# One streamed conditioning product in eight units with a ring of eight loads, its gate product moved into the next stream

## The chip, the cores and the metric

The kernel runs on one core of one Trainium2 chip. The metric is the device time of one execution in microseconds, as the median of several executions. For the kernel before it is 2430.32 us (three runs, 2429.95 to 2431.19).

## The reference, cut to what matters

One layer of a mixed recurrent network is computed for 288 tokens: a prompt of 256 tokens and 8 sequences of 4 sample tokens. All of it is float32, the model width D is 2048.

```python
mod = silu(c) @ ada_w + ada_b                # c: 1 + 8 rows of 2048, ada_w: 2048 x 12288
sh1, sc1, g1, sh2, sc2, g2 = split(mod, 6)
h = rms_norm(x) * (1 + sc1) + sh1
proj = h @ w_in                              # 2048 x 18448: heads q, f, i, g, ..., and 8 + 8 gate columns
...                                          # HGRN2 and mLSTM heads, w_out, residual
h = rms_norm(x) * (1 + sc2) + sh2
...                                          # ConvFFN with w_up and w_down, residual, final norm
```

The change is about the first line for sh1 and sc1 (columns 0 to 4095 of ada_w, 33.6 MB), the first rms_norm, and the product of h with the 16 gate columns of w_in (input and forget gates of the mLSTM heads, C_MI and C_MF).

## The kernel before, in words

**Weights in chunks.** Every weight matrix is streamed once from HBM. A chunk is four contraction tiles of 128 rows by 256 columns (KC = 4, CN = 256): one DMA of 512 KB on SP's queue, in rows of 1 KB, into one of four slots of `raw` (RING = 4). For a chunk of w_in, ACT rounds it to float32r (`hi`, L878, tile `whi`), DVE takes the rest (`lo`, L1239, tile `wlo`), and PE multiplies (`chunk`, L523 to L525): per contraction tile and half of 128 columns three matmuls over 288 tokens, whi with xh, whi with xl, wlo with xh, 24 in all. xh and xl are the two parts of the normalised, modulated input. A `stage` on SP, and a `stream` on PE, ACT and DVE, walk through the same list of kinds: "s" is such a chunk, "a" is a chunk of ada_w for the later conditioning vectors, which goes into `araw` and takes four matmuls (`ada_chunk`, L534: 32 columns of `cs` against 256 columns, one contraction tile in each quarter of the output's partitions). The program's float32 matmuls show as two rows each in the trace.

**The first conditioning product.** Before the first stream, `ada1_stream` takes the 64 chunks for sh1 and sc1 through `raw`: per turn i of 8 eight chunks, four for each of two banks. After four chunks ACT copies the 128 x 256 partial sums out (`ada_rows_of`, L881), PE adds the four quarters with `sel` and transposes (`ada_turn`, L541, two matmuls of 128 columns), and DVE adds the bias (L1254). SP loads chunk k when the chunk four places earlier has been used (`ada1_stage`). In the first four turns PE also transposes the inputs (`xtm`, L502, three per contraction tile, 16 tiles), ACT copies them to `xT` (L949) and squares them (L952), and POOL adds the squares up (L1653). Then one matmul with ones (L629) makes the mean squares, and ACT makes rstd. ACT's queue loads c, x, the parameter rows (`partm`), the gate columns (`gw`), three gate constants and `cvr`, in this order, before its first computation.

**Between this product and the first stream.** When all of mod is there, DVE adds 1 to the scales (L1302) and for each of four groups of contraction tiles multiplies by rstd (L1311) and modulates the samples (L1314, L1316), ACT modulates the prompt (L932) and rounds to xh (L938), and DVE takes xl (L1306). PE then multiplies the 16 gate columns, 8 at a time (L640 to L642, 96 matmuls), and starts the first stream, `stream(hg_base(0), HG_KINDS, A_HG)`, of 40 "s" and 12 "a" chunks. While PE works on its first three chunks, ACT and DVE compute the rows of the gates, which need the gate product (ACT L976 to L986, DVE L1333 to L1356); their loops over the fourth and later chunks come behind these in program order. After the first stream PE transposes the gate rows (L502 on `merged`).

The lines that set the order before the first stream are these:

```python
pe.wait_ge(landed[k % RING], 4 * ada1_base(i)[0] + 16 * (k // RING + 1))
ada_chunk(raw[:, k % RING], s == 0, s == 3, ps[:, b, 0, :], KC * s).then_inc(used, 1)
...
for k in range(8):
    if not first or k >= RING:
        sp.wait_ge(used, ada1_base(i)[0] + k - RING + 1 + FREE)
    load(k, ada_v, KC * (k % 4), 512 * i + CN * (k // 4))
```

Of the kernel before, what the change touches and what calls it, by code (L numbers as in the profile page):

```python
# [21 lines left out]
P = 128  # L22
# [23 lines left out]
CONST_ALL = 37  # L46
SEL_DONE = 11
# [5 lines left out]
CN = 256  # L53

# [15 lines left out]
N_ADA1 = (0, 0)  # L70


# [5 lines left out]
def ada1_base(i):  # L78
    return ahead(N_ADA1, i, 8, 1)


N_HG = (64, 8)
# [36 lines left out]

A_HG = 16  # L120
# [22 lines left out]
HG_TURNS = (2, 11, 20, 29)  # L143
HG_TURNS_ML = (1, 8, 16, 23)
# [14 lines left out]
def build(nc, x_prompt, x_sample, c_prompt, c_sample, state_hgrn, state_mlstm_C, state_mlstm_n, state_mlstm_m,  # L159
# [5 lines left out]
    with ExitStack() as ctx:  # L165
# [8 lines left out]
        whi = sb("whi", [P, RING, KC, CN], F32R)  # L174
        wlo = sb("wlo", [P, RING, KC, CN], F32R)
# [47 lines left out]
        arows1 = sb("arows1", [P, CN], stack=setup)  # L223
        arows = (arows0, arows1)
# [3 lines left out]
        ctm = sb("ctm", [NB, D], stack=setup)  # L228
        cvr = sb("cvr", [2 * FT, NS, P], stack=setup)
        partm = sb("partm", [P, 4, P], stack=setup)  # L230
        gw = sb("gw", [P, KT, 2 * MH], stack=setup)
        gwh = sb("gwh", [P, KT, 2 * MH], F32R, stack=setup)
        gwl = sb("gwl", [P, KT, 2 * MH], F32R, stack=setup)
# [91 lines left out]
        a_used = sem("a_used")  # L325
        ada_rows = sem("ada_rows")
# [5 lines left out]
        par_t, par_c = sem("par_t"), sem("par_c")  # L332
        c_zero, c_silu, c_t, c_c = (sem(n) for n in ("c_zero", "c_silu", "c_t", "c_c"))
        cv_t, cv_c = sem("cv_t"), sem("cv_c")
        x_t, x_c, x_sum = sem("x_t"), sem("x_c"), sem("x_sum")
# [92 lines left out]
        def _(sp):  # L428
# [20 lines left out]
            def ada1_stage(i, first=False):  # L449
                for k in range(8):  # L450
                    if not first or k >= RING:
                        sp.wait_ge(used, ada1_base(i)[0] + k - RING + 1 + FREE)
                    load(k, ada_v, KC * (k % 4), 512 * i + CN * (k // 4))
# [10 lines left out]
            ada1_stage(0, first=True)  # L464
            with sp.Fori(1, 8) as i:
                ada1_stage(i)
# [31 lines left out]
        def _(pe):  # L498
# [38 lines left out]
            def ada_turn(n, half, acc):  # L537

                pe.wait_ge(ada_rows, n + 1)
                for m in range(2):  # L540
                    x = mm(acc[:, CN + NB * m:CN + NB * (m + 1)], arows[half][:, P * m:P * (m + 1)], sel[:, :], start=True, stop=True)  # L541
                x.then_inc(ada_cols, 1)
# [12 lines left out]
            def stream(N, kinds, a0=None, steps=None, length=4, kt0=0, xparts=None, halves=None, a_ring=araw):  # L555

                steps = nothing() if steps is None else steps
                for k, kind in enumerate(kinds):
                    if kind == "s":
# [7 lines left out]
                        chunk(N[0] - N_HG[0] + q + 1, q, s == 0, s == length - 1, b % 2, xh, xl, kt0 + KC * s, steps, halves if q == 0 else None)  # L567
                    else:
                        e = before(kinds, k, "a")
                        if e % 4 == 0:  # L570
                            pe.wait_ge(ada_free, a0 - A_HG + e // 4 + FREE)
                        pe.wait_ge(a_landed[e % ARING], 16 // ARING * before_a(a0) + 16 * (e // ARING + 1))
                        ada_chunk(a_ring[:, e % ARING], e % 4 == 0, e % 4 == 3, ab, KC * (e % 4)).then_inc(a_used, 1)
                    if k >= 2 and kinds[k - 2] == "a" and before(kinds, k - 1, "a") % 4 == 0:
                        ada_turn(a0 + before(kinds, k - 1, "a") // 4 - 1, 0, ab)
                drain(steps)

            def ada1_stream(i, hook=None):

                for k in range(8):  # L580
                    b, s = k // 4, k % 4
                    if s == 0:
                        pe.wait_ge(bank_free[b], ada1_base(i)[1] + FREE)
                    pe.wait_ge(landed[k % RING], 4 * ada1_base(i)[0] + 16 * (k // RING + 1))
                    ada_chunk(raw[:, k % RING], s == 0, s == 3, ps[:, b, 0, :], KC * s).then_inc(used, 1)
                    if s == 1 and b:
                        ada_turn(2 * i, 0, ps[:, 0, 0, :])
                    if hook is not None:
                        hook(k)
                ada_turn(2 * i + 1, 1, ps[:, 1, 0, :])  # L590

# [3 lines left out]
            pe.wait_ge(const, 4)  # L595
            pe.wait_ge(ld_c, 32)
            pe.wait_ge(c_silu, 1)
            for kt in range(KT):
                x = tr(ab[:, NB * kt:NB * (kt + 1)], ctm[0:NB, P * kt:P * (kt + 1)])
            x.then_inc(c_t, 1)  # L600
            pe.wait_ge(ld_par, 16 * 9)
            for t, r in enumerate((128, 92, 88, 108)):
                x = tr(R[:, 2, P * t:P * t + r], partm[0:r, t, :])
            x.then_inc(par_t, 1)

            pe.wait_ge(const, SEL_DONE)
            pe.wait_ge(c_c, 1)
            pe.wait_ge(ld_x, 48)
            for i in range(4):
                def hook(k, i=i):  # L610
                    if k % 2:
                        kt = 4 * i + k // 2
                        pe.wait_ge(x_c, kt + X_FREE - 1)
                        for tt in range(3):
                            w = P if tt < 2 else TS
                            x = tr(R[:, k // 2 % 2, P * tt:P * tt + w], xtm[0:w, tt, P * kt:P * (kt + 1)])
                        x.then_inc(x_t, 1)
                ada1_stream(i, hook)
            pe.wait_ge(ld_conv, 16)
            for g in range(2):  # L620
                if g == 0:
# [1247 lines left out]
```

## Time and profile before

| | us |
|---|---|
| median of three runs | 2430.32 |
| the profiled execution, its own time | 2427.25 |
| its span | 2425.7 |
| granted TensorE clock, mean over the span | 0.966 of full speed |
| PE busy | 2298.0 |

The span is what the instruction records cover; the execution's own time is 1.55 us longer. Times within the profile count from the start of the span. L12 is line 12 of the kernel. "PEld" are weight loads of TensorE. The granted clock has two levels, 0.5 (1.2 GHz) and 1.0 (2.4 GHz); other values are means over a stretch. The share of the DMA engines is the mean over 16 of them of the time that their packets took; packets overlap, so it can be above 1.

### The profile page before, as it was taken

To read this page: it belongs to the slowest core of one execution; us is meant where nothing else is said; L and a number is where in the kernel's file an instruction comes from. 1 tells how busy PE (TensorE), PEld (TensorE's weight loads), DVE (VectorE), ACT (ScalarE), POOL (GpSimd) and SP (SyncE) were. 2 spreads that over 40 slices of the span, in tenths; PEclk is the share of its full clock that TensorE was granted. 3 is DMA by queue.
4 is the path that set the end of the run, shared out by engine and by line. 5 is a ranking of instruction groups with operands and counts; after the bars stand their busy time and mean duration, and the time that the engine had idled before them with its cause. 6 is when DMAs were issued, how large, how long until landed. Compare 5 with 4: busy or idle time off the path is not lost. (4 is left out here: it accounts for less than half of the span.)

```text
span 2425.7 us, 45810 instructions
## 1 busy us (share of the span) xinstructions
PE 2298.0 (95%) x17728; PEld 2101.1 (87%) x17728; DVE 1096.9 (45%) x1443; ACT 1016.2 (42%) x1377; POOL 331.2 (14%) x461
## 2 busy tenths in 40 slices
PE   5769999899899999999999997899999999999997
PEld 2249999899889888888888896899999999999997
DVE  0043446446346444443443555655454545544443
ACT  2244455345435433444343443544444434433332
POOL 2100022112122221112111214000000000010000
PEclk8579999999999999999999999999999999999998
DMA  8947665656566565665765656465666555555552
GB/s 265 303 156 217 198 190 188 194 175 196 174 188 202 173 213 172 199 228 179 236 211 185 193 167 211 149 200 183 197 191 199 186 163 165 184 181 165 163 168 83
DMA packets 425403, 460.15 MB, mean 190 GB/s; under 512 B 16671, under 2 KB 415111, under 8 KB 424029
## 3 DMA queue, kind: packets, MB, share of 16 engines
q1 hardware_dynamic: 410064, 409.26, 53.8%
q0 software_dynamic: 11408, 45.54, 5.7%
q10 hardware_dynamic: 3782, 3.14, 0.4%
q8 instruction: 122, 2.00, 0.3%
q14 instruction: 27, 0.22, 0.0%
HBM read 431.48 MB, written 26.39 MB: 189 GB/s over the span
## 5 line engine op out<-in xcount | busy, mean ns | idle before, releaser
L523 PE MATMUL ps<-xh,whi 128*128 128x288 f32 x3968 | 1203.1, 303 | 39.2 <-issue 28.4
L1239 DVE TENSOR_TENSOR wlo<-raw,whi 128x1024 fp32r<-128x1024 f32 x584 | 734.8, 1261 | 1033.8 <-ACT whi L878 1032.6
L524 PE MATMUL ps<-xl,whi 128*128 128x288 f32 x3968 | 1175.2, 296 | 0.0
L525 PE MATMUL ps<-xh,wlo 128*128 128x288 f32 x3968 | 1174.9, 296 | 0.0
L878 ACT ACTIVATE whi<-raw 128x1024 fp32r<-128x1024 f32 x584 | 615.8, 1057 | 885.3 <-PE ps L525 789.6
L523 PEld LDWEIGHTS ps<-xh,whi 128*128 128x128 f32 x3968 | 749.8, 189 | 110.9 <-issue 94.1
L524 PEld LDWEIGHTS ps<-xl,whi 128*128 128x128 f32 x3968 | 750.1, 189 | 5.9 <-issue 5.9
L525 PEld LDWEIGHTS ps<-xh,wlo 128*128 128x128 f32 x3968 | 749.6, 189 | 0.0
L523 PE MATMUL ps<-ffh,whi 128*128 128x288 f32 x704 | 209.5, 298 | 0.0
L525 PE MATMUL ps<-ffh,wlo 128*128 128x288 f32 x704 | 207.5, 295 | 0.0
L524 PE MATMUL ps<-ffl,whi 128*128 128x288 f32 x704 | 207.2, 294 | 0.0
L523 PEld LDWEIGHTS ps<-ffh,whi 128*128 128x128 f32 x704 | 132.2, 188 | 0.2
L525 PEld LDWEIGHTS ps<-ffh,wlo 128*128 128x128 f32 x704 | 132.1, 188 | 0.0
L524 PEld LDWEIGHTS ps<-ffl,whi 128*128 128x128 f32 x704 | 132.0, 188 | 0.0
L534 PE MATMUL ps<-raw,cs 128*32 128x256 f32 x512 | 61.6, 602 | 21.1 <-DMA raw<-in_ada_w 21.1
L1827 POOL COPY tails<-abuf 128x4 f32 x22 | 4.2, 189 | 446.4 <-ACT abuf L1190 446.4
L534 PE MATMUL ab<-araw,cs 128*32 128x256 f32 x768 | 61.3, 391 | 0.0
L534 PEld LDWEIGHTS ps<-raw,cs 128*32 128x32 f32 x512 | 14.5, 141 | 51.0 <-DMA raw<-in_ada_w 44.1
L1727 POOL TENSOR_TENSOR S<-S,AC 128x1024 f32<-128x1024 f32 x16 | 31.6, 1972 | 164.8 <-PE R L696 164.8
L1254 DVE TENSOR_TENSOR mod<-ps,par 128x18 f32 x16 | 2.8, 176 | 107.3 <-PE ps L541 107.3
L1196 ACT ACTIVATE ffh<-yb 128x576 f32 x22 | 15.1, 686 | 69.0 <-DVE yb L1556 69.0
L1549 DVE SCALAR_TENSOR_TENSOR acv<-abuf,par,acv 128x304 f32<-128x304 f32 x88 | 41.0, 527 | 0.0
(352 smaller groups left out, 1654.6 us busy)
## 6 DMA issues: line engine op xcount, KB each, us to landing
raw<-in_w_in SPq DMA_DIRECT2D x288, 512.0 KB, 4.9
raw<-in_w_up SPq DMA_DIRECT2D x176, 512.0 KB, 3.6
araw<-in_ada_w SPq DMA_DIRECT2D x96, 512.0 KB, 3.9
raw<-in_w_down SPq DMA_DIRECT2D x88, 512.0 KB, 3.6
raw<-in_ada_w SPq DMA_DIRECT2D x64, 512.0 KB, 5.1
raw<-in_w_out SPq DMA_DIRECT2D x32, 512.0 KB, 3.6
araw_up<-in_ada_w SPq DMA_DIRECT2D x32, 512.0 KB, 4.3
S<-in_state_hgrn POOLq DMA_DIRECT2D x16, 512.0 KB, 4.8
```

Of the source, the lines that this page charges most:

```text
L523: mm(o, whi[:, s, kk, cols], hi[:, kt0 + kk, :], start=first and kk == 0, stop=False)
L524: mm(o, whi[:, s, kk, cols], lo[:, kt0 + kk, :], start=False, stop=False)
L525: x = mm(o, wlo[:, s, kk, cols], hi[:, kt0 + kk, :], start=False, stop=last and kk == KC - 1)
L534: x = mm(acc[32 * kk:32 * kk + 32, 0:CN], cs[:, kt0 + kk, :], weights[:, kk, :], start=first, stop=last)
L878: A(whi[:, s], raw[:, s], ACT.Copy).then_inc(hi_done, 1)
L1196: A(ffh[:, bass.ds(2 * i, 2), :], yb[:, :, :], ACT.Copy).then_inc(ff_hi, 1)
L1239: TT(wlo[:, s], raw[:, s], whi[:, s].bitcast(F32), ALU.subtract).then_inc(lo_done, 1)
L1254: TT(mod[:, bass.ds(2 * n, 2), :], acc[:, CN:CN + 2 * NB].rearrange("p (m b) -> p m b", b=NB), rep_last(bias_row[:, bass.ds(2 * n, 2)], NB ...
L1549: STT(acv[:, m, 0:AB - 2], abuf[:, m, w:w + AB - 2], cw[w][:, c1], acv[:, m, 0:AB - 2], ALU.mult, ALU.add).then_inc(ff_conv, 1)
L1727: G(S0[:, :, :], S0[:, :, :], rep_last(AC[:, 3, j, :], P), ALU.mult).then_inc(hg["scaled"], 1)
L1827: nc.gpsimd.tensor_copy(tails[:, bass.ds(2 * i, 2), 0:2], abuf[:, :, TP:TP + 2]).then_inc(ab_tail, 1)
```

## The change

- The product for sh1 and sc1 is taken in 8 units of 512 columns, shift and scale in turn (`unit_tiles`): unit 0 is shift tiles 0 to 3, unit 1 scale tiles 0 to 3, and so on. A unit is eight chunks of the old shape (four contraction tiles by 256 columns, 512 KB, rows of 1 KB), loaded into a new ring of eight, `uraw`, which lies over `whi` and `wlo`; a semaphore counts each pair of chunks. SP loads a pair again when the same pair of the unit before has been used.
- A unit has one copy by ACT of 128 x 512, one turn of four matmuls by PE, and one addition of bias by DVE, with the 1 of the scales in it.
- `raw` is free in this stage. SP issues the first four chunks of the first stream, and the first two "a" chunks, without a wait, behind the last unit.
- PE sums the squares itself: 16 matmuls with ones over 288 tokens, four in each of units 1 to 4, in place of POOL's 16 additions and one matmul.
- The first rms_norm follows the units: DVE multiplies by rstd after unit 3, groups 0 and 1 are modulated after it, group 2 after unit 5, group 3 after unit 7.
- c goes in as rows of 128 values, on SP's queue ahead of the first unit (2 transposes in place of 16); the parameter rows go on SP's queue behind unit 0; the gate columns (now two loads of 8 columns, into columns 0 and 32 of a tile 40 wide), the gate constants and `cvr` go on POOL's queue behind its constants. ACT's queue has only x. `cs` is zeroed by POOL.
- The gate product is 48 matmuls with 40 columns, taken as steps inside the first stream from its chunk 5 on (GATES = 5); ACT and DVE compute the gate rows inside their loops at chunks 9 to 11, 14 and 15.

The diff, cut to its core:

```diff
@@ sync
+            def unit_load(u, c):
+                s = (UC * u + c) % URING
+                if u:
+                    sp.wait_ge(u_used, 4 * (u - 1) + c // 2 + 1)
+                sp.dma_start(uraw[:, s], ada_v[:, KC * (c % 4):KC * (c % 4 + 1), bass.ds(P * unit_tiles(u) + CN * (c // 4), CN)]).then_inc(u_landed[s // 2], 16)
-            ada1_stage(0, first=True)
-            with sp.Fori(1, 8) as i:
-                ada1_stage(i)
+            sp.dma_start(ctm[:, 0, :], c_sample.rearrange("b (k p) -> (b k) p", p=P)).then_inc(ld_c, 16)
+            sp.dma_start(ctm[0:KT, 1, :], c_prompt.rearrange("b (k p) -> (b k) p", p=P)).then_inc(ld_c, 16)
+            for c in range(UC):
+                unit_load(0, c)
...
+            for u in range(1, UNITS):
+                for c in range(UC):
+                    unit_load(u, c)
@@ stage
-                        if first and n < RING:
-                            sp.wait_ge(used, N[0] + n - RING + 1 + FREE)
-                        else:
-                            sp.wait_ge(lo_done, N[0] - N_HG[0] + n - RING + 1)
+                        if not first or n >= RING:
+                            sp.wait_ge(lo_done, N[0] + n - RING + 1)
@@ tensor
+            def unit(u, tiles):
+                acc = ps[:, u % 2, 0, :]
+                if u >= 2:
+                    pe.wait_ge(ada_rows, u - 1)
+                for h in range(UC // 2):
+                    pe.wait_ge(u_landed[h], 32 * (u + 1))
+                    for c in (2 * h, 2 * h + 1):
+                        for kk in range(KC):
+                            x = mm(acc[32 * kk:32 * kk + 32, CN * (c // 4):CN * (c // 4 + 1)], cs[:, KC * (c % 4) + kk, :], uraw[:, c, kk, :], start=c % 4 == 0, stop=c % 4 == 3)
+                    x.then_inc(u_used, 1)
+                    if h == 0 and u:
+                        unit_turn(u - 1)
+                    tiles(h)
+            def squares_sum(g):
+                pe.wait_ge(sq_done, g + 1)
+                for kt in range(4 * g, 4 * g + 4):
+                    x = mm(ab[:, 0:T], ones[:, :], merged[:, kt, :], start=kt == 0, stop=kt == KT - 1)
...
+                    if u == 0 and h == 0:
+                        pe.wait_ge(ld_x, 48)
...
+            def gates(j, o, n, i):
+                pe.wait_ge(gw_lo, 1)
+                pe.wait_ge(small_c, 5)
+                pe.wait_ge(xlo, 4)
                 for kt in range(KT):
...
+                    if kt % 2:
+                        yield
-            pe.wait_ge(cv_c, 2)
-            stream(hg_base(0), HG_KINDS, A_HG)
+            pe.wait_ge(ada_free, UNITS + FREE)
+            stream(hg_base(0), HG_KINDS, A_HG, late(GATES, gates(0, "", 0, 0)), xparts=0)
@@ scalar
+            for u in range(4):
+                unit(u)
+            act.wait_ge(const, 7)
+            root(1, ab[:, 0:T], 1.0 / D)
...
+            unit(4)
...
+            act.wait_ge(ld_gw, 32)
...
+            modulate(1, merged, 0, KT, (0, 1))
+            unit(5)
+            modulate(1, merged, 0, KT, (2,))
+            unit(6)
+            unit(7)
+            hi(N_HG, 0, True)
+            hi(N_HG, 1, True)
+            modulate(1, merged, 0, KT, (3,))
+            hi(N_HG, 2, True)
@@ vector
+            unit(6)
+            unit(7)
+            dve.wait_ge(ada_free, UNITS + FREE)
+            samples(1, merged, 3, 0, KT)
+            lo(N_HG, 0, True)
+            lo(N_HG, 1, True)
+            low_parts(1, merged, 3)
+            lo(N_HG, 2, True)
```

## Rows read from the trace of the kernel before

**Rows 1.** The page's busy times of PE, and its slices of the span.

```profile
PE 2298.0 (95%) x17728; PEld 2101.1 (87%) x17728; DVE 1096.9 (45%) x1443; ACT 1016.2 (42%) x1377; POOL 331.2 (14%) x461
...
PEclk8579999999999999999999999999999999999998
```

**Rows 2.** Busy time, granted clock, DMA share and GB/s in stretches before 200 us.

```profile
core 0: us, PE busy (x) PEld busy (x) DVE busy (x) ACT busy (x) POOL busy (x), PEclk, DMA share, GB/s
0.00:137.00 137.00, 89.24 (x642) 37.56 (x642) 5.75 (x25) 27.66 (x51) 23.04 (x60) 0.67 0.90 288
95.00:135.00 40.00, 30.87 (x220) 10.88 (x224) 1.06 (x6) 2.31 (x6) 0.00 (x0) 0.50 1.00 324
10.00:15.00 5.00, 0.00 (x0) 0.00 (x0) 0.00 (x0) 0.00 (x0) 2.33 (x10) 1.00 1.04 286
...
80.00:85.00 5.00, 2.29 (x14) 1.10 (x18) 2.18 (x6) 3.05 (x6) 3.66 (x5) 0.50 0.46 176
...
190.00:200.00 10.00, 10.00 (x80) 9.42 (x79) 4.90 (x4) 4.24 (x4) 0.00 (x0) 1.00 1.09 355
```

**Rows 3.** The timeline at the end of the conditioning product, up to the first stream.

```profile
137.34 0.25 PEld L534 LDWEIGHTS ps<-raw,cs 128*32 128x32 f32 x8 [0.60 <-DMA raw<-in_ada_w]
138.54 0.39 ACT L881 ACTIVATE arows<-ps 128x256 f32<-128x256 f32 x1 [6.54 <-PE ps L534]
138.98 1.02 PE L541 MATMUL ps<-sel,arows 128*128 128x9 f32 x4 [0.51 <-ACT arows L881]
...
152.60 0.40 PE L640 MATMUL R<-xh,gwh 128*8 128x288 f32 x1 [12.60 <-DVE xl L1306]
...
155.20 0.33 PE L642 MATMUL R<-xh,gwl 128*8 128x288 f32 x1
...
168.91 0.29 PE L523 MATMUL ps<-xh,whi 128*128 128x288 f32 x1
```

**Rows 4.** Groups of one engine's instructions by line: PE from 150 us, ACT and DVE before 180 us.

```profile
L641 PE MATMUL R<-xl,gwh 128*8 128x288 f32 x32 | 10.0, 313 | 0.0
L932 ACT ACTIVATE merged<-merged,mod 128x256 f32<-128x256 f32 x16 | 8.3, 587 | 2.9 <-DVE merged L1311 2.9
L878 ACT ACTIVATE whi<-raw 128x1024 fp32r<-128x1024 f32 x4 | 4.2, 1052 | 1.8 <-DMA raw<-in_w_in 1.8
L1239 DVE TENSOR_TENSOR wlo<-raw,whi 128x1024 fp32r<-128x1024 f32 x3 | 3.7, 1226 | 1.1 <-ACT whi L878 1.1
L1314 DVE TENSOR_TENSOR merged<-merged,mod 128x128 f32<-128x128 f32 x4 | 1.2, 292 | 0.1
```

**Rows 5.** The timeline around PE's stall in the first stream, and at its end.

```profile
178.56 0.64 PE L534 MATMUL ab<-araw,cs 128*32 128x256 f32 x8
181.59 0.40 PE L523 MATMUL ps<-xh,whi 128*128 128x288 f32 x1 [2.39 <-DVE wlo L1239]
...
310.97 0.72 PE L502 MATMUL R<-ident,merged 8*128 8x8 f32 x9
```

**Rows 6.** The chain that ended last, later in the kernel: one period of three chunks.

```profile
1535.38 0.57 PE ab L534 x8
...
1545.71 0.57 PE ab L534 x8
```

**Rows 7.** The timeline of PE's pieces of work during the conditioning product.

```profile
26.39 0.93 PE L502 MATMUL R<-ident,xtm 128*128 128x128 f32 x3
...
82.72 1.30 PE L629 MATMUL R<-lnms,ones 128*128 128x288 f32 x2 [3.24 <-POOL lnms L1653]
83.94 3.42 PE L534 MATMUL ps<-raw,cs 128*32 128x256 f32 x32
```

**Rows 8.** DMA issues by line: KB each, and us from issue to landing.

```profile
raw<-in_ada_w SPq DMA_DIRECT2D x64, 512.0 KB, 5.1
...
xT_spill<-xT POOLq DMA_DIRECT2D x2, 1152.0 KB, 6.5
gw<-in_w_in ACTq DMA_DIRECT2D x1, 128.0 KB, 10.9
```

More of the change, by code:

```diff
@@ L45 @@
 ROW_T = ROW_WK
-CONST_ALL = 37
-SEL_DONE = 11
+CONST_ALL = 39
+CONST_CS = 1
+SEL_DONE = 12
 X_FREE = 2
@@ L325, in build @@
         a_used = sem("a_used")
+        u_landed = [sem(f"u_landed{i}") for i in range(URING // 2)]
+        u_used = sem("u_used")
         ada_rows = sem("ada_rows")
@@ L574, in stream @@
                     if k >= 2 and kinds[k - 2] == "a" and before(kinds, k - 1, "a") % 4 == 0:
-                        ada_turn(a0 + before(kinds, k - 1, "a") // 4 - 1, 0, ab)
+                        ada_turn(a0 + before(kinds, k - 1, "a") // 4 - 1, ab)
                 drain(steps)
[L578 to L590, printed above, removed]
@@ L593, in _ @@
             pe.sem_inc(used, FREE)
             pe.sem_inc(a_used, FREE)
-            pe.wait_ge(const, 4)
+            pe.wait_ge(const, 5)
             pe.wait_ge(ld_c, 32)
[L597 to L603, printed above, removed]
@@ L604, in _ @@
-            x.then_inc(par_t, 1)
-            pe.wait_ge(const, SEL_DONE)
[L607 to L612, printed above, removed]
+            pe.wait_ge(c_silu, 2)
+            tr(ab[:, 0:P], ctm[:, 0, :])
+            tr(ab[:, P:P + KT], ctm[0:KT, 1, :]).then_inc(small_t, 1)
+            pe.wait_ge(const, SEL_DONE)
+            pe.wait_ge(small_c, 2)
@@ L613, in hook, with tiles @@
+            for u in range(UNITS):
+                def tiles(h, u=u):
+                    if u == 0 and h == 0:
+                        pe.wait_ge(ld_x, 48)
+                    if u < 4:
+                        kt = 4 * u + h
                         pe.wait_ge(x_c, kt + X_FREE - 1)
@@ L791, in ml_step, with late @@
                     yield
-            pe.wait_ge(cv_c, 2)
-            stream(hg_base(0), HG_KINDS, A_HG)
+            def late(k0, step):
+                while now[0] < k0:
+                    yield
+                yield from step
+            pe.wait_ge(ada_free, UNITS + FREE)
+            stream(hg_base(0), HG_KINDS, A_HG, late(GATES, gates(0, "", 0, 0)), xparts=0)
             pe.wait_ge(row_d, ROW_T)
@@ L964, in _ @@
-            act.wait_ge(const, 6)
-            root(1, R[:, 0, 0:T], 1.0 / D)
-            with act.Fori(4, 8) as i:
-                ada1(i, False)
-            for k in range(LEAD):
-                hi(N_HG, k)
-            modulate(1, merged, 0, KT)
-            r = merged[0:MH]
-            act.wait_ge(gmm, 1)
-            act.wait_ge(ld_gs, 48)
-            act.wait_ge(xlo, 4)
-            A(r[:, 0, :], R[0:MH, 0, 0:T], ACT.Identity, bias=gb[:, 0:1]).then_inc(row_a, 1)
-            A(r[:, 1, :], R[0:MH, 1, 0:T], ACT.Identity, bias=gb[:, 1:2]).then_inc(row_a, 1)
@@ L1288, in _ @@
             TT(gwl[:, :, :], gw[:, :, :], gwh[:, :, :].bitcast(F32), ALU.subtract).then_inc(gw_lo, 1)
-            with dve.Fori(4, 8) as i:
-                ada1_stream(i)
-            for k in range(LEAD):
-                lo(N_HG, k)
+            low_parts(1, merged, 0)
+            low_parts(1, merged, 1)
+            unit(5)
+            dve.wait_ge(ada_free, 6 + FREE)
+            samples(1, merged, 2, 0, KT)
+            low_parts(1, merged, 2)
+            unit(6)
[6 more added lines that the diff above has]
+            lo(N_HG, 2, True)
             def modulate(nth, src, tmp, shift, scale):
```

411 lines of the change are left out of this document (225 added, 186 removed).

## The prediction

> **What bounds the kernel now.** I read the page first. PE is busy for 95% of the span, and the granted clock is at full speed in nearly every slice, except at the very start [rows 1]. The views by stretch come next. In the first 137 us PE is busy for 89 us at a mean clock of 0.67, while the DMA engines have a share of 0.90, and of 1.00 between 95 and 135 us, where they move 324 GB/s [rows 2]. So there are two kinds of time: a start of some 137 us that the loads of ada_w set, and 2290 us behind it that PE sets. What is saved ahead of PE's first product stays saved, because nothing behind it waits for a fixed hour, and what is added to PE behind it is paid in full.
>
> Between the two lies a third piece. The last chunk of ada_w has landed at 137.3, the first product of the first stream starts at 168.9 [rows 3]. These 31.6 us hold the last turn, the modulation of all four groups, which DVE and ACT do only then, and 96 gate matmuls. The DMA engines have nearly nothing to do in it, since the four slots of raw are full. Last, PE stalls for 2.4 us in the stream's fourth chunk, behind DVE's gate rows [rows 5].
>
> **The change, part by part.** All is set against the profiled execution: span 2425.7, its own time 2427.25, which is 3.07 under the median of the runs. That offset is added at the end.
>
> A. *The last load lands earlier.* The bytes stay the same, in the same pieces of 1 KB. In 137 us at a share of 0.90 the engines did 123.3 us of work at a share of 1.00 [rows 2]; about 1.5 of these were for the first stream's chunks, and the first load can't land before 1 or 2 us. The idle tenth came from four slots whose release hung on PE, which itself began late (ACT was busy issuing DMAs) and waited for POOL's sums: 80 to 85 us has a share of 0.46 [rows 2]. With eight slots, c issued first, and no visit to POOL, I take the engines as busy throughout: last landing at 123 in place of 137.3, 14.3 less. Bounds: 137 (no gain, if the idle tenth stays) and 112, which is 39 MB at the 355 GB/s of 190 to 200 us [rows 2]. I take 123, since 95 to 135 is the same traffic and shows 324 at a share of 1.00.
>
> The Trainium skill, DMA: Bandwidth & Descriptors, section Bandwidth, says to make transfers 1 MiB or larger, and gives 341 GB/s for 1 MB pieces; the loads here stay at 512 KB. By the 341 the last landing would be near 116, and the sum 7 us lower; it is counted under the fast rival below.
>
> PE must keep up for this. At half clock a chunk costs 0.86 (32 rows, four chunks, in 3.42) and a tile's transposes 0.86 to 0.93 [rows 7]; a unit's turn is two of the old, 2.0 [rows 3]; four square matmuls at 1.3 each are 5.2 or less [rows 7]. A unit is 6.9 + 2.0, and units 1 to 3 have 3.5 + 4.8 more: some 17 us at half clock, against 4.2 MB at 324 GB/s = 12.9 us for its loads. At full clock it is 9. So even at half clock PE falls behind by about 4 us in each of units 1 to 3, which eight slots can hold for the most part, and catches up in units 5 to 7 (9 against 12.9). Followed pair by pair, I come to a last landing of 120 to 125. The copies, squares and additions of ACT and DVE in a unit are under 5 us and lie beside PE; without that cover they would cost these 5 us once. The two spill stores (6.5 us to landing [rows 8]) are the same bytes as before.
>
> B. *From the last landing to the first product.* On the path now lie: the last pair of chunks on PE 1.9 (four took 3.42 [rows 7]); ACT's copy of 512 columns, 0.39 for 256 [rows 3], so 0.7; the turn of four matmuls, 2.0; DVE's bias add 0.2; the samples of group 3, two at 0.29 [rows 4]; DVE's lo of chunk 0, 1.23 [rows 4]; some 0.4 of hand-overs. That is 7.0 in place of 31.6: 24.6 less. ACT's hi of chunk 0 (1.05 [rows 4]) runs beside the turn, and its data is there: raw was free, and the chunk lands about 1.6 us after the last of ada_w. Groups 0 to 2 are modulated in units 4 to 6, hidden by loads of 12.9 us each. Group 3 is late next: after two hi at 1.05, four activations at 0.59 busy and a rounding at 1.2, then DVE's xl at 1.35, it is ready some 10 us after the last landing. Only chunk 3 needs it, at 7.0 + 3 x 3.25 = 16.8. Bounds: 5 (turn and pair at full clock) and 12 (if chunk 0 had to wait for a load of 5.1 [rows 8]).
>
> C. *The gate product inside the stream.* PE does a period of three chunks and one "a" chunk in 10.33, the "a" chunk is 0.57 [rows 6], so a chunk is 3.25 and a matmul 0.136. 48 gate matmuls are 6.5 more in the stream. The 96 of before [rows 4] are within the 31.6 already. No bound is far from this: the moving side is 288 columns in both.
>
> D. *PE starts at the lower clock.* From 95 to 135 the clock is at 0.5 [rows 2], and the first gate matmuls keep that pace until 155.2, 2.6 us after the first [rows 3]. At the start of the stream the same costs about half of the stretch at the lower level: 1.4. Bounds 0 and 4.
>
> E. *The stall behind the gate rows goes.* The first stream takes 142.1 us from 168.91 to 310.97 [rows 3, 5]. 40 chunks at 3.25, 12 "a" chunks at 0.57 and three turns at 0.5 are 138.5; 3.6 is lost now, the stall of 2.4 and the slower matmuls behind it. In the changed kernel the rows are computed in loops whose lo and hi are three chunks ahead: at chunk 9 ACT has 3.7 us and DVE 2.6 us of rows, against 3 x 3.25 of lead. I take 3.6 less; bounds 0 and 3.6.
>
> F. *Costs of nothing*: more unrolled instructions; the parameter rows on SP's queue between units 0 and 1 (nine short issues, while eight loads are in flight); the two gate loads on POOL's queue, 10.9 to landing now [rows 8], needed by ACT only after unit 4, near 85 us; POOL's stores of the gate states, later by a few us, for which nobody waits before the first heads.
>
> Sum: -14.3 - 24.6 + 6.5 + 1.4 - 3.6 = -34.6. 2427.25 - 34.6 = 2392.7, and with the offset of 3.07 **2395.7 us**.
>
> **The rivals.**
> 1. *PE paces the units.* At half clock PE's work of the stage is 64 chunks x 0.86 + 32 turn matmuls x 0.5 + 16 tiles x 0.9 + 16 squares x 1.3 = 106 us, and it can't pass its first tile before x has landed, near 16. For it: only 0.67 of the clock was granted, and the squares are new on PE. Against it: three units are light, and denser work brought the full clock at 155 [rows 3]. With some waits for ACT it ends near 131, 8 us later: 2404.
> 2. *The loads go faster.* With eight in flight, 341 to 355 GB/s and the full clock at the end: 7 to 10 us less, 2387. The best 10 us show 355 [rows 2], no stretch of this stage does for long.
> 3. *Slower than before: small pieces on POOL's queue slow all loads.* The gate columns become 4096 pieces of 32 bytes beside `cvr` and the constants, drained by the same 16 engines as ada_w, with ACT waiting for them ahead of the modulation. The only slice with such pieces moved 286 GB/s at a share of 1.04 [rows 2]. The price is 39 MB over the rate: at 286 the last landing is at 137. The change comes out slower only when it is later than 158, a mean rate under 250 GB/s, or when the gate loads land after about 120 us. At 240 GB/s the time would be 2435. 10.9 us to landing for half the pieces [rows 8] speaks against it.
> 4. *The change does not do what it says*: the engines were already full (a share of 1.00 at 324 GB/s), and the gates, rows and modulation only move into places where PE or the loads wait for them. Then A gives nothing, B ends at 20 and each move is paid: 2425 to 2430.
>
> The Trainium skill, DMA: Bandwidth & Descriptors, section Issuing engines are not separate DMA queues, says that all queues end in the same 16 engines, so moving loads between queues saves issue time only. By it the moves to SP and POOL give no bandwidth, and rival 3's pieces do take from ada_w. I count no gain from the moves beyond PE's earlier start.
>
> **How the numbers follow.** My forecast (last landing 119 to 127) has 0.64, rival 1 0.18, rival 2 0.11, rival 3 0.03, rival 4 0.04. The predicted time is that of the first. Its own range is 2390 to 2401; with rivals 1 and 2 and the bounds of B and D it is 2385 to 2409. A measurement can tell about 0.2%, 4.9 us, from no change. Faster 0.93, same 0.03, slower 0.04.
>
> **What would show it.** In the changed profile: the last matmul on `uraw` near 123 to 125; a DMA share of 0.98 or more from 5 to 120; the first product on `whi` near 130; 48 gate matmuls within chunks 5 to 7; no PE idle over 1 us in the first stream; the `merged` transposes of its end near 276 in place of 310.97. I am wrong if the last `uraw` matmul is past 130 with PE busy (rival 1), if PE waits for loads at a share of 1.00 and a low rate (rival 3), or if the start is early and the time comes back later as idle in the stream.

## The result, and the profile after

The changed kernel takes **2388.8 us** in the median of four runs (2384.35 to 2389.88), beside 2430.76 (2429.95 to 2432.68) for the kernel before on the same chip. The ratio is 0.9823, 95% interval 0.9806 to 0.9840: faster by 1.8%. The forecast was 2395.7 with a range of 2385 to 2409, so the time lies inside the range, 6.9 us below the number.

Busy times and slices of the changed kernel's page:

```profile
span 2386.8 us, 45374 instructions
...
PE 2288.2 (96%) x17696; PEld 2106.7 (88%) x17696; DVE 1092.8 (46%) x1433; ACT 1012.0 (42%) x1370; POOL 324.1 (14%) x452
...
PEclk8699999999999999999999998999999999999998
```

PE does 10 us less than before [rows 1] and the span is 38.9 us shorter. Most of the rest was idle time at the start: ahead of the transposes of `merged` at the end of the first stream PE stood idle for 39.8 us, and for 65.2 before. The views by stretch show where (same columns as [rows 2]):

```profile
0.00:137.00 137.00, 97.20 (x740) 56.05 (x741) 23.16 (x39) 42.55 (x71) 17.32 (x52) 0.74 1.05 328
...
20.00:30.00 10.00, 2.06 (x23) 0.93 (x19) 0.00 (x0) 0.41 (x1) 0.00 (x0) 0.70 1.14 191
...
30.00:120.00 90.00, 74.82 (x591) 39.12 (x587) 14.02 (x29) 29.38 (x51) 2.55 (x3) 0.69 1.10 355
95.00:120.00 25.00, 18.98 (x156) 8.76 (x160) 2.91 (x6) 4.43 (x7) 0.00 (x0) 0.57 1.10 348
```

The kernel before, over the same 90 us:

```profile
30.00:120.00 90.00, 67.88 (x492) 28.03 (x484) 4.30 (x18) 21.72 (x40) 13.99 (x18) 0.59 0.94 308
```

From 30 to 120 us the engines move 355 GB/s at a share of 1.10, where the kernel before had 308 at 0.94, and 324 at 1.00 between 95 and 135 us [rows 2]. So a share of 1.00 was not full. In the ten microseconds from 20 on the rate falls to 191 at a share of 1.14: the engines are busy, and little arrives.

The timeline from the last two chunks of ada_w to the first product of the stream (compare [rows 3]):

```profile
119.12 1.93 PE L622 MATMUL ps<-uraw,cs 128*32 128x256 f32 x16 [1.05 <-DMA uraw<-in_ada_w]
...
121.12 0.60 ACT L985 ACTIVATE urows<-ps 128x512 f32<-128x512 f32 x1 [12.22 <-PE ps L622]
121.61 1.99 ACT L930 ACTIVATE whi<-raw 128x1024 fp32r<-128x1024 f32 x2
...
121.77 1.88 PE L633 MATMUL ps<-sel,urows 128*128 128x9 f32 x8 [0.72 <-ACT urows L985]
123.69 0.20 DVE L1323 SCALAR_TENSOR_TENSOR mod<-ps,par 128x36 f32<-128x36 f32 x1 [9.45 <-PE ps L633]
...
124.45 2.35 DVE L1292 TENSOR_TENSOR wlo<-raw,whi 128x1024 fp32r<-128x1024 f32 x2
...
125.82 0.58 PE L547 MATMUL ps<-xh,whi 128*128 128x288 f32 x1 [2.17 <-DVE wlo L1292]
...
127.22 1.36 DVE L1350 TENSOR_TENSOR xl<-merged,xh 128x1152 fp32r<-128x1152 f32 x1 [0.41 <-ACT xh L970]
...
129.79 0.34 PE L548 MATMUL ps<-xl,whi 128*128 128x288 f32 x1
```

Pair, copy, turn, bias, samples, lo: the forecast's path, item by item. The matmuls take 0.44 us until 129.79 and 0.29 from 129.97 on, so the lower clock lasts 4 us of the stream.

The transposes of `merged` at the end of the first stream (instances, min/median/max ns, first and last start; compare the last row of [rows 5]):

```profile
L526 PE MATMUL R<-ident,merged x9: 200/201/224, 272.1 to 272.6; 8*128 8x8 f32 x9
```

That gives the balance of the change. The last landing is read at PE's start: of the last chunk before, of the last pair after.

| piece | before | after | measured | forecast |
|---|---|---|---|---|
| start to the last landing (A) | 137.34 | 119.12 | -18.2 | -14.3 |
| last landing to first product (B) | 31.57 | 6.70 | -24.9 | -24.6 |
| first product to `merged` transposes (C, D, E) | 142.06 | 146.3 | +4.2 | +4.3 |
| behind the transposes | 2114.7 | 2114.7 | 0.0 | 0 |
| span | 2425.7 | 2386.8 | -38.9 | -34.6 |

The start of these transposes, 272.1, is the figure that most experiments are read by. Nothing behind it was changed by any of them, and in two measurements of the changed kernel it repeated far better than the time (last experiment). Where the landing itself is compared, differences of up to 1.4 us are not clear of scatter (see the last section).

### The profile page after: what moved, and what is told of

It is laid out like the page before. It is cut to its first block and busy times, and to the rows that moved or that the text cites. A ratio compares the mean times of both kernels' runs of the same rounds, so it can differ in the third digit from the quotient of the medians.

```text
span 2386.8 us, 45374 instructions
## 1 busy us (share of the span) xinstructions
PE 2288.2 (96%) x17696; PEld 2106.7 (88%) x17696; DVE 1092.8 (46%) x1433; ACT 1012.0 (42%) x1370; POOL 324.1 (14%) x452
## 5 line engine op out<-in xcount | busy, mean ns | idle before, releaser
L622 PE MATMUL ps<-uraw,cs 128*32 128x256 f32 x512 | 50.3, 529 | 28.2 <-DMA uraw<-in_ada_w 27.9
L622 PEld LDWEIGHTS ps<-uraw,cs 128*32 128x32 f32 x512 | 17.1, 138 | 49.5 <-DMA uraw<-in_ada_w 24.6
L1472 DVE SCALAR_TENSOR_TENSOR Sst<-Sst,AC,R 128x128 f32<-128x128 f32 x112 | 39.0, 348 | 4.0
```

The source lines that it names most:

```text
L622: x = mm(acc[32 * kk:32 * kk + 32, CN * (c // 4):CN * (c // 4 + 1)], cs[:, KC * (c % 4) + kk, :], uraw[:, c, kk, :], start=c % 4 == 0, sto ...
L1472: STT(Sst[:, c, :], Sst[:, c - 1, :], AC[:, 2, j, c:c + 1], u_of(c), ALU.mult, ALU.add).then_inc(hg["state"], 1)
```

## The experiments

Theory: the ring of eight keeps the DMA engines full, so that the loads alone set the last landing (A); B is a chain of short steps; the moved gate work is paid as C, D and E say. Rivals: A comes from elsewhere (who releases slots, how small pieces share the engines, PE's pace), or a move costs or saves something else.

### 1. Four loads in flight, released in pairs

```diff
-                if u:
-                    sp.wait_ge(u_used, 4 * (u - 1) + c // 2 + 1)
+                if 4 * u + c // 2 >= 2:
+                    sp.wait_ge(u_used, 4 * u + c // 2 - 1)
```

> The changed kernel with at most four loads of ada_w in flight instead of eight (SP waits for the pair two places back); nothing else differs. Theory A (eight in flight raise the rate of the loads: 348 GB/s at a share of 1.10 in the changed kernel, 324 at 1.00 before): the rate between 30 and 120 us falls to about 324 GB/s, the last matmul on uraw starts near 128 instead of 119, and the time is about 2397 us (8 to 9 more). Rival (the earlier first load and PE's freedom from POOL gave the gain, the depth nothing): rate stays at 345 or more, time within 2 us of the changed kernel's 2388.8.

Measured: 2412.57 against 2430.66, ratio 0.9923 (0.9907 to 0.9940). The last pair of `uraw` starts at 146.1 (119.1 in the changed kernel), the transposes come at 299.9. The stretch from 30 to 120 us:

```profile
30.00:120.00 90.00, 67.29 (x459) 36.00 (x455) 11.69 (x24) 25.53 (x45) 2.55 (x3) 0.63 0.81 268
```

The share falls to 0.81 and the rate to 268 GB/s. The depth matters, and three times as much as expected: 27.8 us at the transposes (23.8 in the median time) in place of 8 or 9. That is worse than the four slots of before, which had 308 over the same 90 us; runs 10 and 11 take it apart.

### 2. The gate product ahead of the stream

```diff
-            stream(hg_base(0), HG_KINDS, A_HG, late(GATES, gates(0, "", 0, 0)), xparts=0)
+            drain(gates(0, "", 0, 0))
+            stream(hg_base(0), HG_KINDS, A_HG, xparts=0)
```

> The changed kernel with its 48 gate matmuls ahead of the first stream instead of inside it from chunk 5 on. They need all four groups of xl, ready at 128.6 in the changed kernel, so the first product on whi moves from 125.8 to about 136 (6.5 of gate matmuls, about 1 for the lower clock), and the stream is 6.5 shorter: the transposes of the gate rows at the end of the first stream move from 272.1 to about 275.5, time about 2392 us (3 to 4 more). Rival (what counts is only that 96 matmuls became 48, the place is worth nothing): 272 and 2389.

Measured: 2391.15, ratio 0.9840 (0.9823 to 0.9856); first `whi` product at 137.6, transposes at 275.7, 3.6 later than 272.1. PE's wait ahead of the gates (us in total, times, longest):

```profile
PE R L679 <- DVE xl L1351: 5.1, 1, 5.1
```

The 48 gate matmuls are done in either place; ahead of the stream PE also stands still until the fourth group of `xl` is there, which inside it is hidden by chunks 0 to 2. Of these 5.1 us the changed kernel has 2.2 at the same place too, waiting for `wlo`, so the longer wait costs 2.9. The last pair of `uraw` started 0.5 later here (119.6); that leaves 0.2 of the 3.6. The rival, that the place is worth nothing, falls.

### 3. The gates and their rows ahead

```diff
-                gate_rows(q)
+            gate_rows(9)
+            gate_rows(14)
...
-            def hook(q):
-                gate_rows(q)
+            for q in (9, 10, 11, 15):
+                gate_rows(q)
```

(on top of run 2; the first part is in ACT's program, the second in DVE's.)

> As e2_gates_ahead, and ACT and DVE compute the gate rows ahead of their loops, as the kernel before does. If the stall in the fourth chunk (2.4 us and 1.2 us of matmuls at the lower clock behind it) came from DVE's gate rows, it is back: transposes at the end of the first stream 3.6 us later than in e2_gates_ahead (about 279), time about 2395.5 us. Rival (the stall came from the loads of the fourth chunk, not from the rows): no idle time of PE in the stream, same as e2_gates_ahead.

Measured: 2394.86, ratio 0.9854 (0.9838 to 0.9871); transposes at 280.7, 5.0 later than in run 2. The stall of before is back, behind DVE, at 151.29, four chunks into the stream:

```profile
PE ps L547 <- DVE wlo L1294: 2.7, 1, 2.7
```

2.7 us of stall where [rows 5] had 2.39. Behind it 13 matmuls start 0.24 us apart in place of 0.13, until 154.75: the lower clock again, some 1.5 us. The remaining 0.7 lies ahead of the stream, whose first product comes at 138.3 here and at 137.6 in run 2. Within the stream the gate rows cost 4.3 us: E is a real term.

### 4. The whole modulation behind the last unit

```diff
-            modulate(1, merged, 0, KT, (0, 1))
             unit(5)
-            modulate(1, merged, 0, KT, (2,))
             unit(6)
             unit(7)
-            hi(N_HG, 0, True)
-            hi(N_HG, 1, True)
-            modulate(1, merged, 0, KT, (3,))
-            hi(N_HG, 2, True)
+            for k in range(LEAD):
+                hi(N_HG, k, True)
+            modulate(1, merged, 0, KT)
```

(DVE's samples and low parts move in the same way.)

> The changed kernel with all four groups modulated behind the last unit (the first rms_norm's product with rstd stays early). If the order of the stream needs only group 0 at its start and one group per chunk: the first product moves from 125.8 to about 129.6 (three hi, one group on ACT at 3.2, xl at 1.4), no further stall, time about 2392.5 us (3 to 4 more). Rival (all of modulation is on the path, as its 14 us were before): PE waits for xl at chunks 1 to 3 too, and the time is 10 or more above 2388.8.

Measured: 2391.46, ratio 0.9843 (0.9826 to 0.9859); transposes at 277.3, 5.2 later. PE's largest wait at the start of the stream:

```profile
PE ps L547 <- DVE xl L1347: 7.4, 1, 7.4
```

PE waits 7.4 us for group 0 instead of 2.2 for `wlo`. The first product comes at 130.2, 4.4 later, and the lower clock lasts 5.9 us of the stream in place of 4, which costs the other 0.8. Of B's 24.9 us, then, only some 4 to 5 come from modulating groups 0 to 2 early. The larger part is the gate product: before, it took PE from 152.60 to 168.91, 16.3 us between the last landing and the first product [rows 3].

### 5. The sum of squares on POOL

```diff
-                    if 1 <= u <= 4 and h == 1:
-                        squares_sum(u - 1)
+                    if u == 4 and h == 1:
+                        pe.wait_ge(x_sum, KT)
+                        mm(ab[:, 0:T], ones[:, :], lnms[:, :], start=True, stop=True).then_inc(ms_done, 1)
```

(POOL adds the 16 tiles of `merged` into `lnms`, as before the change.)

> The changed kernel with the squares summed by POOL's 16 additions and one matmul again. Theory (the loads pace the units: PE waits 27.9 us for them in the changed kernel): last matmul on uraw within 1 us of 119.1, time within 1.5 us of 2388.8. Rival 1 of the prediction (PE paces the units): PE has about 10 us less to do in units 1 to 4, the last matmul on uraw comes 3 or more earlier. Third possibility (POOL's sums hold the rms_norm back, as they held PE in the kernel before): later, by up to 4.

Measured: 2384.89 against 2428.53, ratio 0.9822 (0.9805 to 0.9838); transposes at 272.4. PE has 2 matmuls for the sum in place of 32 and waits longer for loads (34.8 us up to 130 us, 27.9 in the changed kernel), and the landing does not move (119.3). In the changed kernel PE does not pace the loads. The median is 3.9 us lower than the first one of the changed kernel, outside the 1.5 expected; the kernel before, run beside each, is 2.2 lower too.

### 6. The gate columns in 64-byte pieces

```diff
-                for g in range(2):
-                    pool.dma_start(gw[:, :, 32 * g:32 * g + MH], win_v[:, :, C_MI + MH * g:C_MI + MH * (g + 1)]).then_inc(ld_gw, 16)
+                pool.dma_start(gwc[:, :, :], win_v[:, :, C_MI:C_MI + 2 * MH]).then_inc(ld_gw, 16)
...
+                nc.gpsimd.tensor_copy(gw[:, :, 32 * g:32 * g + MH], gwc[:, :, MH * g:MH * (g + 1)]).then_inc(gw_in, 1)
```

> The changed kernel with the gate columns loaded once in 2048 pieces of 64 bytes (as in the kernel before) and spread by two copies on POOL, instead of 4096 pieces of 32 bytes. From 20 to 30 us the changed kernel moves 191 GB/s at a share of 1.14, 4.5 us of load time less than at its 348. Theory (the number of small pieces makes this trough): it is about half as deep, last matmul on uraw about 2 us earlier (117), time 2386.5 to 2387. Rival (the trough is made by cvr, the parameter rows or the restart of the ring): no change.

Measured: 2384.93, ratio 0.9827 (0.9809 to 0.9845); transposes at 273.7, 1.6 later where 2 earlier was expected. The trough is shallower all the same:

```profile
20.00:30.00 10.00, 4.19 (x32) 1.46 (x25) 0.00 (x0) 0.41 (x1) 0.52 (x2) 1.00 1.14 221
30.00:60.00 30.00, 27.78 (x207) 15.05 (x206) 0.83 (x5) 8.83 (x19) 0.00 (x0) 0.94 1.06 341
```

### 7. No gate columns at all

```diff
-                    pool.dma_start(gw[:, :, 32 * g:32 * g + MH], win_v[:, :, C_MI + MH * g:C_MI + MH * (g + 1)]).then_inc(ld_gw, 16)
+                    nc.gpsimd.memset(gw[:, :, 32 * g:32 * g + MH], 0.01).then_inc(ld_gw, 1)
```

The gate weights are a constant here: the load of the 16 gate columns of w_in is left out.

> The changed kernel with no load of the gate columns at all (the gate weights are a constant, so the gates and all that hangs on them are not the reference's; the same instructions run otherwise). It prices the loads of small pieces by themselves: if they make the trough of 20 to 30 us, the rate there is above 300 GB/s and the last matmul on uraw starts about 4 us earlier (115); if not, under 1 us.

Measured: 2387.36, ratio 0.9825 (0.9804 to 0.9846); transposes at 275.4, 3.3 later where 4 earlier was expected. Three stretches of this kernel:

```profile
20.00:30.00 10.00, 4.76 (x38) 2.11 (x30) 0.00 (x0) 1.31 (x3) 0.00 (x0) 0.71 1.14 261
55.00:60.00 5.00, 4.17 (x55) 1.92 (x54) 0.00 (x0) 2.17 (x4) 0.00 (x0) 1.00 0.84 270
70.00:75.00 5.00, 3.82 (x49) 2.31 (x51) 0.00 (x0) 2.47 (x4) 1.17 (x2) 1.00 0.76 227
```

The small pieces do make part of the trough: 261 GB/s without them, 191 with them, though not the 300 that was expected. But the share, which stays at 1.10 in the changed kernel, falls to 0.84 and 0.76 later. Who holds the loads up there? The wait of SP's queue for PE in this kernel, up to 130 us (us in total, times, longest):

```profile
SPq L462 <- PE ps L622: 43.5, 23, 7.5
```

and PE's squares in it (min/median/max ns, first and last start):

```profile
L639 PE MATMUL ab<-merged,ones x32: 406/687/848, 37.4 to 79.4; 128*128 128x288 f32 x32
```

The same two of the changed kernel:

```profile
SPq L462 <- PE ps L622: 24.5, 24, 3.9
```

```profile
L639 PE MATMUL ab<-merged,ones x32: 406/406/849, 40.0 to 78.0; 128*128 128x288 f32 x32
```

The squares took 0.687 us each in the median, against 0.406. The granted clock is 0.50 while the first three groups of squares run in this kernel. From one unit's turn to the next PE took 14.6, 13.6 and 13.6 us, against 12.0 for 4.2 MB at 350 GB/s (13.3, 10.5 and 12.4 in the changed kernel), and SP had to wait for slots. That this is the cause was a guess at this point; runs 8 and 9 put it to the test by taking the squares off PE. In run 6 the first group of squares was as slow (4.2 us for four tiles, 2.8 in the changed kernel), but the granted clock shows 1.00 there, so why it was slow is open.

### 8. Runs 5 and 6 together

> Both edits at once: POOL adds the squares (one matmul of ones left on PE), and the 16 gate columns come in one load of 64-byte pieces. Theory (the shallower trough between 20 and 30 us is worth its bytes, 0.3 MB or 0.9 us at 348 GB/s, and was lost in e6 because PE's matmuls of the squares met the lower clock and held the release of slots up): SP's waits for PE at 21 us or less, last uraw matmul near 119.5, first whi product near 125, merged transposes near 271.5, the time 1 us under after. Rival (the later dips of the load rate in e6 have nothing to do with PE's squares): merged transposes near 273.7, as in e6.

Measured: 2381.97 (2379.63 to 2387.47, five runs) against 2430.86, ratio 0.9800 (0.9783 to 0.9818); transposes at 271.2. SP's wait for PE is 22.9 us (21 or less was expected), and in the rows of the loads nothing dips any more:

```profile
20.00:30.00 10.00, 3.23 (x33) 1.22 (x21) 0.00 (x0) 0.41 (x1) 0.81 (x3) 0.65 1.16 218
30.00:120.00 90.00, 69.14 (x557) 33.26 (x555) 15.10 (x29) 29.14 (x51) 15.23 (x19) 0.63 1.10 354
```

### 9. Runs 5 and 7 together

The gate weights are a constant again.

> POOL adds the squares, and the gate columns are not loaded at all (their weights are a constant, which leaves that part of the computation out). This prices the small pieces cleanly. Theory: 20 to 30 us moves 261 GB/s or more in place of 191, 0.7 MB, so the last uraw matmul is 2 us sooner, near 118, first whi product near 124, merged transposes near 270, and no slice between 50 and 80 us has a DMA share under 0.95. Rival (dips not from PE's squares): the share falls again to 0.8 between 55 and 75 us and merged transposes stay near 275.4, as in e7.

Measured: 2382.65 against 2430.86, ratio 0.9804 (0.9787 to 0.9820); transposes at 270.1.

```profile
20.00:30.00 10.00, 4.70 (x42) 2.26 (x34) 0.00 (x0) 0.88 (x3) 0.00 (x0) 0.75 1.13 258
55.00:60.00 5.00, 4.07 (x46) 2.40 (x46) 0.20 (x1) 1.70 (x4) 3.17 (x4) 1.00 1.11 349
70.00:75.00 5.00, 5.00 (x34) 2.35 (x38) 0.20 (x1) 1.04 (x1) 2.77 (x5) 0.50 1.10 350
```

For the first product and the transposes the theory of each holds to a few tenths (the last pair of run 8 starts at 118.3, not 119.5), and the rivals fall. With the squares off PE, the two stretches that had fallen to 0.84 and 0.76 stay at 1.10 or more, and each step out of the trough is worth about its bytes: 272.4 with the two 32-byte loads, 271.2 with the one of 64-byte pieces, 270.1 with none (1.2 and 2.3 us, against 0.7 and 1.9 by the bytes). With the squares on PE the same edits had cost 1.6 and 3.3. So the 4096 pieces of 32 bytes cost some 2.3 us; the 1.2 by itself is not clear of the scatter of the start. And PE is close to pacing the units, as rival 1 said.

### 10. Four in flight, each released by itself

```diff
-                if u:
-                    sp.wait_ge(u_used, 4 * (u - 1) + c // 2 + 1)
+                if UC * u + c >= 4:
+                    sp.wait_ge(u_used, UC * u + c - 3)
...
-                    pe.wait_ge(u_landed[h], 32 * (u + 1))
                     for c in (2 * h, 2 * h + 1):
+                        pe.wait_ge(u_landed[c % 4], 16 * (2 * u + c // 4 + 1))
```

> Four loads of ada_w in flight as in e1, but each slot is released and each load is awaited by itself, not in pairs: the release as it was before the change. Theory (the release in pairs is what starved the queue in e1): 30 to 120 us moves 310 to 324 GB/s, last uraw matmul near 130, first whi product near 136, merged transposes near 283, time near 2400. Rival (the depth alone sets it, four loads cannot fill the queue beside PE's other work): 268 to 285 GB/s, last uraw matmul near 145, merged transposes near 297, time near 2411.

Measured: 2403.13, ratio 0.9895 (0.9875 to 0.9915); the first `whi` product at 141.2, transposes at 287.7.

```profile
30.00:120.00 90.00, 71.82 (x507) 35.40 (x507) 13.73 (x28) 28.67 (x50) 2.55 (x3) 0.68 0.91 299
```

299 GB/s: between the two expectations, and 12.2 us earlier than run 1. Of the 27.8 us that run 1 lost, the pairs made 12.2 and the depth of four made 15.6. The last chunk starts at 135.4 here, only 2.0 before the 137.3 of the kernel before, with every other part of the change in place: 16.2 of A's 18.2 us are the depth. Between 95 and 120 us this kernel also shows the rate of the kernel before:

```profile
95.00:120.00 25.00, 17.80 (x152) 6.52 (x152) 12.51 (x21) 12.93 (x22) 1.38 (x1) 0.66 1.01 325
```

(ACT and DVE wait for the end of the whole last unit here before they write `whi` and `wlo`, since the semaphore counts chunks.)

### 11. Six in flight, released in pairs

```diff
-                if u:
-                    sp.wait_ge(u_used, 4 * (u - 1) + c // 2 + 1)
+                if 4 * u + c // 2 >= 3:
+                    sp.wait_ge(u_used, 4 * u + c // 2 - 2)
```

> Six loads of ada_w in flight, released in pairs (three pairs in place of four). Theory (beyond what covers landing and PE's jitter, more depth gives nothing; e1 with two pairs lost 27 us): 30 to 120 us moves 335 to 345 GB/s, last uraw matmul near 123, first whi product near 129, merged transposes near 275, time 2 to 4 us over after. Rival (the time follows the number in flight in proportion): 308 GB/s, last uraw matmul near 132, merged transposes near 285.

Measured: 2392.84, ratio 0.9847 (0.9828 to 0.9866); transposes at 274.6, 2.5 after those of the changed kernel.

```profile
30.00:120.00 90.00, 71.48 (x563) 37.62 (x555) 14.11 (x29) 29.37 (x51) 2.55 (x3) 0.78 1.04 341
```

4, 6 and 8 in flight, in pairs, give 268, 341 and 355 GB/s: nearly all of the gain is had with six.

### 12. The changed kernel once more

> The changed kernel once more, not a line different, to learn how much of a difference between two kernels its own runs show. In its first profile the merged transposes start at 272.1 and 2114.7 us lie behind them. Theory (the start is set by the loads and repeats; behind it, how often the granted clock drops for some 3 us differs from run to run and moves the rest by up to 5 us either way): merged transposes at 271.5 to 274, behind them 2105 to 2115, median 2384 to 2390. Rival (the part behind repeats within 1 us for the same code, and the 6.8 us by which the median with the squares on POOL and the 64-byte load lies lower are that kernel's own): behind the transposes 2114 to 2116, median 2388 to 2390.

Measured: 2388.70 (2385.56 to 2391.55, five runs) against 2427.43, ratio 0.9838 (0.9824 to 0.9851).

```profile
L526 PE MATMUL R<-ident,merged x9: 200/202/225, 272.2 to 272.8; 8*128 8x8 f32 x9
```

The transposes come 0.1 us from where they came the first time. Behind them lie 2389.7 - 272.2 = 2117.5 us against 2114.7, a little past the end of what was expected. So the part behind does not repeat to the microsecond, but the median did: 2388.7 and 2388.8.

The combination of run 8 has the lowest median of the study, 48.9 us under the kernel before that ran beside it; the changed kernel is 42.0 and 38.7 under it in its two measurements. The interval 0.9783 to 0.9818 lies below the second one of the changed kernel, 0.9824 to 0.9851, but overlaps the first, 0.9806 to 0.9840: that run 8 is faster is likely and not shown. Only 1.0 us of its lead stands ahead of the transposes. Where the rest of the 6.8 us between the medians comes from is open (see the last section).

## Why the prediction was right, and where it was off

**A, the last landing: -18.2 in place of -14.3. This is the step that was mis-sized.** Its mechanism is shown: with four in flight the landing is 16.2 to 27.0 us later (runs 10, 1), and with PE relieved it does not move (run 5). The price was taken from 95 to 135 us of before, "324 at a share of 1.00", as the rate of full engines. It was the rate of four loads in flight: run 10, with four, shows 325 at 1.01 between 95 and 120 us, and the changed kernel, with eight, 348 at 1.10. The row that told the truth was beside it: 190 to 200 us, 355 GB/s at a share of 1.09 [rows 2]. A share of 1.00 is not a ceiling when a slice elsewhere shows 1.09. The rate belongs to rival 2, though not the full clock at the end that it added (0.57 between 95 and 120 us); its 2387 was 1.8 us from the time, and the forecast's own range of 2390 to 2401 missed it by 1.2. So the wide range held because it counted rival 2 in. The bound of 112 was not reached for two reasons. The trough of 20 to 30 us, 191 in place of 355 GB/s, is 1.6 MB, or 4.6 us; the first 20 us, with 305 GB/s, are some 2.8 more. Of the trough's 4.6, 2.3 are the gate columns (run 9 against run 5). The other pieces in that stretch (`cvr`, the parameter rows) were not taken out.

The Trainium skill, DMA: Bandwidth & Descriptors, section Specifications, puts the limit of HBM for one core at about 358 GB/s. This trace lies close to it: 347 to 356 in every 5 us from 30 to 120, but for 393 and 400 between 70 and 80 us, just after the two spill stores are issued (68.2 and 68.8). Whether that limit is what holds the rate there, no run shows. The same page's rule to make transfers 1 MiB or larger (section Bandwidth) was weighed in the prediction with its 341 GB/s: eight 512 KB loads in flight gave more than that, so here the number in flight did what the size was to do.

**B: -24.9 in place of -24.6.** Every item of the path stands in the timeline within 0.2 us. 16.3 us of it are the gate product that left, and run 4 prices the early modulation at 4.4 us up to the first product.

**C, D and E together: +4.2 in place of +4.3.** Run 2 splits them, since its stream has neither gate matmuls nor a stall nor the lower clock: 138.1 us from the first product to the transposes. The kernel before took 142.1, so E is 4.0 where 3.6 was forecast (4.3 in run 3). The changed kernel takes 146.3, so C and D are 8.2 where 7.9 was forecast. D, estimated at 1.4, is 4 us of matmuls at 0.24 a piece instead of 0.136, some 1.7 us lost, which leaves C its 6.5. That the sum came out within 0.1 is two errors of 0.3 to 0.4 that cancel.

**F: not quite nothing.** No wait of PE for the parameter rows or the code shows on the path behind the last landing. The gate loads on POOL's queue cost some 2.3 us, not zero. The Trainium skill, DMA: Bandwidth & Descriptors, section Issuing engines are not separate DMA queues, says that DMAs issued on any engine run on the same 16 DMA engines and interleave; by it rival 3's pieces take from ada_w. The traces agree, with 191 GB/s against 258 to 261 when they are gone. At its worst, from 20 to 25 us, the rate is 147 GB/s, half of the 286 that rival 3 took from a slice of before; but the stretch is short. Rival 3's mechanism exists, but it needed a landing past 158 to decide, 39 us later than the one measured.

**Rival 1, PE paces the units,** is false in the changed kernel (run 5), and it decides in run 7, which differs only by a load that isn't there: 3.3 us later, and earlier again when the squares are off PE (run 9). The sum "17 us of PE at half clock against 12.9 of loads" was too large on both sides, 13.6 to 14.6 against 12.0 in run 7, but its sign was right. Which level of the clock the squares meet differs between kernels that differ by a few microseconds at the start.

**Rival 4** is false: the gates (run 2), the rows (run 3) and the modulation (run 4) each lose 3.6 to 5.2 us when moved back. Of the marks, the `uraw` end (119 to 121, not 123 to 125), the first product (125.8, not 130) and the transposes (272.1, not 276) are all early by A's 4 us; the gates are in chunks 5 to 7, and PE never stands idle in the first stream (busy for 146.3 of 146.3 us). A share of 0.98 or more from 5 to 120 us was met, 1.10 on the mean, and said less than was thought: the trough has 1.14 with 191 GB/s.

**The offset.** 3.07 us were added since before's profiled execution lay that much under its median. After's lies 0.2 under its own. The offset was one execution's scatter, and adding it moved the forecast away from the result by 3 of the 6.9 us; A's 3.9 is nearly all of the rest.

## What to carry to other kernels

Read the rate of a load stage from the densest stretch of the whole trace, not from the stage that is to be fixed: there a share of 1.00 may only be the rate of too few loads in flight. Count slots in units of their release: four slots released in pairs moved 268 GB/s, released singly 299. And where an engine comes near the loads' pace, take its optional work off it before anything is tuned on the loads, or a gain there turns into a loss.

## What the runs showed that was not expected

**The start scatters little, the rest more.** The same program put its transposes at 272.1 and 272.2 in two measurements (its last pair of `uraw` at 119.1 and 119.5). In runs 2 and 3, whose edits lie behind that pair, it came at 119.6 and 120.5, so the start is good to some 1.4 us. Meanwhile the part behind them took 2114.7 and 2117.5, and 2104.4 to 2117.5 over all kernels with identical code there. PE's idle time there is 54.4 to 60.1 us in the changed kernel and runs 1 to 12. The granted clock differs more. A stretch of the changed kernel in which PE has just stood still for most of 2 us:

```profile
1326.00:1328.00 2.00, 0.61 (x4) 0.64 (x5) 2.00 (x2) 2.00 (x3) 0.00 (x0) 0.99 0.98 332
1328.00:1330.00 2.00, 2.00 (x11) 2.00 (x10) 2.00 (x3) 2.00 (x4) 0.00 (x0) 0.50 0.41 139
1330.00:1332.00 2.00, 2.00 (x12) 2.00 (x12) 0.96 (x1) 0.42 (x1) 1.46 (x1) 0.66 0.03 8
```

It runs at 1.2 GHz for some 3 us afterwards. The 50 us around it, in the changed kernel and then in run 6, where this drop did not come though the code is the same:

```profile
1300.00:1350.00 50.00, 46.26 (x320) 42.57 (x320) 25.44 (x33) 25.65 (x32) 9.62 (x8) 0.97 0.55 175
```

```profile
1300.00:1350.00 50.00, 46.29 (x338) 41.65 (x338) 26.02 (x34) 26.05 (x38) 11.92 (x8) 1.00 0.52 161
```

Summed over slices of 10 us from the transposes to the end (one minus the granted clock, times the length), the clock takes 27.5 us from the changed kernel and 18.9 from run 6. Runs 6 and 3 have the smallest sums (18.9 and 20.7) and the two shortest parts behind (2104.4 and 2106.7); the others lie at 23.9 to 32.8 and 2110.7 to 2117.5, in no order. So these drops go with the scatter, and are not all of it. Run 8's lead behind the transposes is not explained by them: its sum is 27.7.

**Twice the loads in flight, 1.7 times the time to land.** Eight in flight raised the time from issue to landing of a 512 KB load of ada_w from 5.1 us [rows 8] to 8.7:

```profile
uraw<-in_ada_w SPq DMA_DIRECT2D x64, 512.0 KB, 8.7
...
xT_spill<-xT POOLq DMA_DIRECT2D x2, 1152.0 KB, 10.8
```

So twice the loads in flight gave only some 1.2 times the rate (308 to 355 GB/s from 30 to 120 us); the rest of the depth is time in the queue. The spill stores, 6.5 us before, pay for it too, and nobody waits for them at the start.
